# FFN1 of two token groups in one pass over the weights, FFN2 one pass later, output gates before decay gates

## The reference, cut to what matters

```python
def reference(x, ...):                       # x: 16 x 2048 x 1024, float32
    # macaron half-step FFN before mixing (FFN1, hidden width 2816)
    h = rms_norm(x, ffn1_norm[l])
    x = x + 0.5 * swiglu(h, ffn1_w_gate[l], ffn1_w_up[l], ffn1_w_down[l])
    # two head groups from one projection
    h = rms_norm(x, mix_norm[l])
    proj = h @ w_in[l]
    fq, fk, fv, ff, gq, gk, gv, g_low, g_out = jnp.split(proj, split_idx, axis=-1)
    log_f = jax.nn.log_sigmoid(ff + fox_forget_bias[l])
    fox = fox_attention(fq, fk, fv, log_f)                 # 8 heads, causal, over all earlier frames
    log_a = jax.nn.log_sigmoid(g_low @ gla_w_gate_up[l] + gla_gate_bias[l]) / 16
    gla = gla_chunk_causal(gq, gk, gv, log_a)              # 4 heads, chunks of 64, a running state
    gla = rms_norm(gla, gla_out_norm[l]) * jax.nn.silu(g_out)
    x = x + jnp.concatenate([fox, gla], axis=-1) @ w_out[l]
    # macaron half-step FFN after mixing (FFN2)
    h = rms_norm(x, ffn2_norm[l])
    x = x + 0.5 * swiglu(h, ffn2_w_gate[l], ffn2_w_up[l], ffn2_w_down[l])
    return rms_norm(x, final_norm)
```

## Time and profile before

| | |
|---|---|
| median of 6 runs | 2874.18 us (2869.43 to 3200.55) |
| profiled execution | 2870.64 us |
| its span on the slowest core | 2869.1 us (cores 2850.7 to 2869.1 us) |
| TensorE busy | 2678.3 us, 93% of the span, 13328 matmuls |
| VectorE, ScalarE, GpSimd busy | 1468.1, 1103.9, 250.8 us |
| mean granted TensorE clock, cores 0 to 7 | 0.981 to 0.985 |
| moved by DMA | 423.20 MB; read from HBM 451.09 MB, written 59.77 MB |

### The profile page before, as it was taken

The page is one execution under the profiler, slowest core; times in us unless marked ns, Lnnn a source line. Parts: engine busy times, 40 slices in busy tenths (PEclk is TensorE's granted clock), DMA queues, the critical chain, the costliest instruction groups (busy, mean ns, idle before and its releaser), DMA issues.

```text
span 2869.1 us, 40029 instructions; the slowest of 8 cores (2850.7 to 2869.1 us)
## 1 busy us (share of the span) xinstructions
PE 2678.3 (93%) x13328; PEld 1262.1 (44%) x13328; DVE 1468.1 (51%) x2186; ACT 1103.9 (38%) x2189; POOL 250.8 (9%) x518
## 2 busy tenths in 40 slices
PE   5989888898899999999999999999999999999998
PEld 2435434443345444544445444454444544544443
DVE  3353772582445554456444863547444566455443
ACT  1231431461224732267322531326323375277211
POOL 1111211120000100001000100001000010001000
PEclk9999999999999999999999999999999999999999
DMA  8888769869777454433444354442644423433453
GB/s 182 137 162 157 159 136 184 175 169 222 181 181 191 123 187 145 140 107 121 157 138 141 121 156 167 129 139 89 199 144 136 129 93 125 143 93 126 136 170 115
DMA packets 128166, 423.20 MB, mean 148 GB/s; under 512 B 14799, under 2 KB 14944, under 8 KB 127072
## 3 DMA queue, kind: packets, MB, share of 16 engines
q1 hardware_dynamic: 95920, 308.34, 32.9%
q0 software_dynamic: 31760, 111.26, 22.0%
q10 hardware_dynamic: 288, 1.05, 0.1%
HBM read 451.09 MB, written 59.77 MB: 178 GB/s over the span
## 4 chain that ended last, share of the span: by engine, by line
PE 76%; DMA 10%; DVE 8%; issue 4%; ACT 2%; POOL 0%; DVEq 0%; SPq 0%; ACTq 0%; POOLq 0%
PE bank L303 76%; DMA mixw_t<-mixw 4%; DMA wgu<-wgu 2%; DVE hF L343 2%; DVE hM L740 2%; DVE x_sb L343 1%; DMA wgu<-wgus 1%; DVE Sst L343 1%; DMA wd<-wd 1%; DVE hM L343 1%; DVE Sbf L340 1%; ACT L328 1%; DVE thF L343 1%; DMA wgus<-wgu 1%; DMA mixws<-mixw_t 1%
## 5 line engine op out<-in xcount | busy, mean ns | idle before, releaser
L303 PE MATMUL bank<-hF,wgu 128*128 128x512 bf16 x5632 | 1297.3, 384 | 73.7 <-DMA wgu<-wgu 27.6
L303 PEld LDWEIGHTS bank<-hF,wgu 128*128 128x128 bf16 x5632 | 548.4, 99 | 743.0 <-issue 128.2
L303 PE MATMUL bank<-act,wd 128*128 128x512 bf16 x2816 | 648.8, 381 | 29.5 <-DVE x_sb L343 22.7
L328 ACT ACTIVATE thF<-bank 128x512 f32<-128x512 f32 x352 | 209.7, 598 | 847.0 <-PE bank L303 846.0
L343 DVE SCALAR_TENSOR_TENSOR thF<-thF,bank 128x512 f32<-128x512 f32 x352 | 240.9, 686 | 509.1 <-ACT thF L328 506.8
L328 ACT ACTIVATE hM<-bank,biasT 128x256 bf16<-128x256 f32 (+1 forms) x1152 | 437.8, 472 | 126.6 <-PE bank L303 126.1
L303 PEld LDWEIGHTS bank<-act,wd 128*128 128x128 bf16 x2816 | 272.3, 98 | 362.8 <-issue 52.2
L340 DVE TENSOR_TENSOR act<-bank,thF 128x512 bf16<-128x512 f32 x352 | 242.6, 689 | 188.3 <-PE bank L303 182.6
L343 DVE SCALAR_TENSOR_TENSOR x_sb<-bank,x_sb 128x512 f32<-128x512 f32 x256 | 173.7, 689 | 319.2 <-PE bank L303 318.0
L740 DVE RECIPROCAL hM<-bank 64x128 f32<-64x128 f32 x256 | 244.4, 955 | 52.0 <-PE bank L303 35.1
L340 POOL TENSOR_TENSOR hM<-hM,mask 128x128 bf16<-128x128 bf16 x256 | 118.4, 475 | 1514.9 <-ACT hM L328 1514.5
(11 more groups left out here) (92 smaller groups left out, 1260.3 us busy)
## 6 DMA issues: line engine op xcount, KB each, us to landing
wgu<-wgus SPq DMA_DIRECT2D x264, 512.0 KB, 3.5
wd<-wds SPq DMA_DIRECT2D x192, 352.0 KB, 3.1
wgu<-wgu POOLq DMA_DIRECT2D x88, 512.0 KB, 7.4
mixw_t<-mixws SPq DMA_DIRECT2D x88, 512.0 KB, 3.4
wd<-wd POOLq DMA_DIRECT2D x64, 352.0 KB, 6.7
wgus<-wgu SPq DMA_DIRECT2D x44, 512.0 KB, 5.4
mixw_t<-mixw POOLq DMA_DIRECT2D x40, 512.0 KB, 7.7
wds<-wd SPq DMA_DIRECT2D x32, 352.0 KB, 5.6
```

The costliest lines, as they stand in the source:

```text
L303: ins = e.matmul(out, lhsT=l, rhs=r, start=s0, stop=s1)
L328: ins = e.activation(out=out, in_=in_, func=func, **kw)
```

## The change

FFN1 of groups 0 and 1 becomes one pass (`ffn1_pair`). `ffn` takes a list of lanes (input, activation buffers, group); each weight tile is loaded once and used for every lane. The pair's second lane keeps its input `hF2` and activations `act2` in the tensor `V` (the attention's values, not used before mixer 0), so the fill of V's constant columns moves behind the pair. In the pair's first half the first three tiles are done for lane 0, then for lane 1, and from there on by turns. `x` of group 1 is loaded behind group 0's, and its sums of squares are taken ahead of the pair. Both mixers 0 and 1 then stand behind the pair, and the passes go f1(2), f2(0), f2(1), f1(3), f2(2), ... as before from there on.

`LOADW` now stores every FFN1 tile and every mixer chunk at its first use; FFN2 is as before. Only the first down tile of a half is cut into 10 and 1, and its parts are no longer woven with the second tile's. In the mixer, the four projections of the output gate (chunks 0 and 1) stand ahead of the decay gates.

```diff
@@ build_nc
+        flat = V[:].rearrange("p a b c -> p (a b c)")
+        hF2 = flat[:, 0:8 * T].rearrange("p (k t) -> p k t", k=8)
+        act2 = flat[:, 8 * T:(8 + NC2) * T].rearrange("p (k t) -> p k t", k=NC2)
...
-        MSET(V[:, :, :, 64:128], 1.0, [("V", p, g) for p in range(4) for g in range(4)], eng="dve")
@@ LOADW
-        def LOADW(tag, wb, tile, src, keep, i, first, reads=()):
+        def LOADW(tag, wb, tile, src, keep, i, spread, reads=()):
...
-            kept_at = first + i % 2
+            kept_at = i % 2 if spread else 0
@@ ffn
+        def ffn(f, lanes, middle):
+            pair = len(lanes) == 2
             for half in range(2):
+                todo = [(c, L) for c in range(NC2) for L in lanes]
+                if pair and half == 0:
+                    todo = [(c, L) for L in lanes for c in range(3)] + todo[6:]
+                where = {}
+                for cl, L in todo:
+                    if cl not in where:
+                        where[cl] = wb = nxt("wgu", 3)
+                        LOADW("wgu", wb, wgu[:, wb, :], wgu_d[f], wgu_s[f], half * NC2 + cl, f,
+                              [("x", 0, 5)] if cnt["wgu"] <= 3 else ())
+                    wb = where[cl]
...
-                load(0)
-                load(1)
-                part(0, 0, NC2 - 1)
-                part(1, 0, NC2 - 1)
-                part(0, NC2 - 1, NC2)
-                evac(0)
-                part(1, NC2 - 1, NC2)
-                evac(1)
...
+                for d in range(8):
+                    wb = nxt("wd", 4)
+                    LOADW("wd", wb, wd[:, wb, :], wd_d[f], wd_s[f], half * 8 + d, f, [("act", 5)] if cnt["wd"] <= 4 else ())
+                    for L in lanes:
+                        b = ring[n % 2]
+                        n += 1
+                        for c0, c1 in ([(0, NC2 - 1), (NC2 - 1, NC2)] if d == 0 else [(0, NC2)]):
+                            MM(banks[b][:], [(wd[:, wb, c * 128:(c + 1) * 128], L.act[:, c, :]) for c in range(c0, c1)],
...
+                        STT(x_sb[:, L.xb, d, :], banks[b][:], 0.25, x_sb[:, L.xb, d, :], ALU.mult, ALU.add, [],
+                            [PS(b), ("x", L.xb, d)], level=0)
@@ ffn1_pair
+            norm_h(0, 0, rstdF[:], "rstdF", hF, "hF", 0.5)
+            norm_h(1, 0, rstdM[:], "rstdM", hF2, "hF2", 0.5)
+            ffn(0, [Lane(0, hF, "hF", act, "act", sums(0, sqF, "sqF"), 6),
+                    Lane(1, hF2, "hF2", act2, "act2", sums(1, sqM, "sqM"), 7)], middle)
+            norm_rstd(rstdM[:], "rstdM", 6, 0)
+            norm_h(0, 1, rstdM[:], "rstdM", hM, "hM", 0.5)
+            norm_rstd(rstdF2[:, 1], ("rstdF2", 1), 7, 0.5)
+            MSET(V[:, :, :, 64:128], 1.0, [("V", p, g) for p in range(4) for g in range(4)]
+                 + [("hF2", k) for k in range(8)] + [("act2", c) for c in range(NC2)], eng="dve", level=0.7)
@@ mixer: the loop over chunks 0 and 1 (output gates) moves from behind biasT to ahead of zb
-                LOADW("mixw", wb, mixw[:, wb, :], mixw_d, mixw_s, i, 1, [("act", 10)] if cnt["mix"] <= 2 else ())
+                LOADW("mixw", wb, mixw[:, wb, :], mixw_d, mixw_s, i, 0, [("act", 10)] if cnt["mix"] <= 2 else ())
@@ the order of the passes
-        order = [("f1", 0), ("f1", 1)]
-        for g in range(NTG - 3):
+        P.level = 2
+        ffn1_pre(0, 2, sqF, "sqF", rstdF[:], "rstdF")
+        load_x(1, [("x", 0, 7)])
+        ffn1_pre(1, 3, sqM, "sqM", rstdM[:], "rstdM")
+        load_x(2, [("act", 8)])
+        ffn1_pair(pre(2))
+        P.level = 1
+        mixer(0)
+        norm_h(1, 1, rstdF2[:, 1], ("rstdF2", 1), hM, "hM", 0.5)
+        mixer(1)
+        order = [("f1", 2), ("f2", 0)]
+        for g in range(1, NTG - 3):
             order += [("f2", g), ("f1", g + 2)]
...
-            m = g if kind == "f1" and g < NTG - 1 else NTG - 1 if (kind, g) == ("f2", NTG - 3) else None
+            m = {("f2", 0): 2, ("f2", NTG - 3): NTG - 1}.get((kind, g), g if kind == "f1" and 2 < g < NTG - 1 else None)
```

More of the change, by code:

```diff
@@ L456, in ffn @@
                     STT(thF[:, r, :], thF[:, r, :], 1.0, banks[bg][:], ALU.add, ALU.mult, [], [PS(bg), ("th", r)], level=0)
-                    TT(act[:, cl, :], banks[bu][:], thF[:, r, :], ALU.mult, [("th", r)], [PS(bu), ("act", cl)], level=0)
+                    TT(L.act[:, cl, :], banks[bu][:], thF[:, r, :], ALU.mult, [("th", r)], [PS(bu), (L.atag, cl)], level=0)
                 ring = [(bu + 1) % 3, (bu + 2) % 3]
                 cnt["fb"] = bu + 1
[L460 to L478, removed]
@@ L480, in ffn @@
-                load(0)
-                load(1)
-                part(0, 0, NC2 - 1)
-                part(1, 0, NC2 - 1)
-                part(0, NC2 - 1, NC2)
-                evac(0)
-                part(1, NC2 - 1, NC2)
-                evac(1)
[L488 to L493, removed]
-            return bu
+                n = 0
@@ new lines, in ffn @@
+                for d in range(8):
[6 more added lines that the diff above has]
+                            MM(banks[b][:], [(wd[:, wb, c * 128:(c + 1) * 128], L.act[:, c, :]) for c in range(c0, c1)],
+                               [("wd", wb)] + [(L.atag, c) for c in range(c0, c1)], [PS(b)], start=(c0 == 0),
+                               stop=(c1 == NC2))
+                        STT(x_sb[:, L.xb, d, :], banks[b][:], 0.25, x_sb[:, L.xb, d, :], ALU.mult, ALU.add, [],
+                            [PS(b), ("x", L.xb, d)], level=0)
+                        if half == 1:
+                            L.after(d, bu if L.bank is None else L.bank)
+                    if d == 1 and half == 0 and middle is not None:
+                        middle(bu)
@@ L496, in ffn1, with sums @@
+            return bu
+        def sums(xb, sq, tag):
+            return lambda d, b: norm_sq(xb, d, sq, tag, b, d == 7, 0)
         def ffn1(tg, middle):
@@ L498, in ffn1, with ffn1_pair, load_x, ffn1_pre @@
             norm_h(xb, 0, rstdF[:], "rstdF", hF, "hF", 0.5)
-            b = ffn(0, xb, lambda d, b: norm_sq(xb, d, sqF, "sqF", b, d == 7, 0), middle)
+            b = ffn(0, [Lane(xb, hF, "hF", act, "act", sums(xb, sqF, "sqF"))], middle)
             norm_rstd(rstdM[:], "rstdM", b, 0)
             norm_h(xb, 1, rstdM[:], "rstdM", hM, "hM", 0.5)
-        def load_x(tg):
-            xb = tg % 3
[L505 to L512, removed]
+        def ffn1_pair(middle):
+            norm_h(0, 0, rstdF[:], "rstdF", hF, "hF", 0.5)
[7 more added lines that the diff above has]
+                 + [("hF2", k) for k in range(8)] + [("act2", c) for c in range(NC2)], eng="dve", level=0.7)
+        def load_x(tg, reads=()):
+            xb = tg % 3
+            DMA("sp" if tg < 3 else "pool", ("x", xb, tg < 3), x_sb[:, xb, :, :].rearrange("p k t -> p (k t)"), x_d[tg],
+                1 << 21, reads=reads, writes=[("x", xb, k) for k in range(8)], slack=8000.0)
+        def ffn1_pre(tg, b, sq, tag, rstd, rtag):
             for k in range(8):
-                norm_sq(xb, k, sqF, "sqF", b, k == 7, None)
-            norm_rstd(rstdF[:], "rstdF", b, None)
+                norm_sq(tg % 3, k, sq, tag, b, k == 7, None)
+            norm_rstd(rstd, rtag, b, None)
         def ffn2(tg, middle):
@@ L563, in mixer, with ev @@
             ACTV([(fa, fa, AF.Exp, None, -1.0)], [], ["fa"])
+            for i in range(2):
+                w3, wk = chunk(i)
+                for hh in range(2):
+                    h = 2 * i + hh
+                    def ev(b, h=h):
+                        ACTV([(t1f, banks[b][:], AF.Tanh, None, 0.5)], [], [PS(b), ("sqM", 0), ("sqM", 1)])
+                        STT(cc[:, 4 + h, :], t1f, 1.0, banks[b][:], ALU.add, ALU.mult, [("sqM", 0), ("sqM", 1)],
+                            [PS(b), ("cc", 4 + h)])
+                    proj_T(w3, wk, hh * 128, ev)
             zb = []
@@ L611, in mixer @@
                    ALU.subtract, ["fref"] + [("nFs", g) for g in range(tg + 1)], [("biasT", t)])
[L612 to L619, removed]
-                            [PS(b), ("cc", 4 + h)])
-                    proj_T(w3, wk, hh * 128, ev)
             w3, wk = chunk(2)
```

24 lines of the change are left out of this document (11 added, 13 removed).

## The result

The changed kernel takes 2782.04 us (median of 10 runs, 2776.89 to 3228.09) against 2874.92 (median of 20) of the kernel before on the same chip: ratio 0.9671, 95% interval 0.9644 to 0.9698. The forecast was 2788. Executions in which a die ran at a lower clock are in the medians and ranges but not in the ratios; one experiment (the rewoven down tiles) had too few others for a ratio, so two single times stand for it. The profiled execution took 2784.26 us, its span 2782.3 on core 1.

What follows compares the result with a forecast made beforehand. TensorE was taken as the bound. Loss up to f1(3)'s end falls from 169 to 91.5 us; that 77.5 and 8 behind it take 2870.6 to 2785, median 3.5 above: 2788 us, range 2745 to 2845.

Steps and rivals of the forecast that it cites:

- Start of the pair: Up to the end of lane 1's first three tiles at 56.6 us: loss 35 us, bounds 27 and 54.
- with all eight behind it I add 4: Pair's start: all eight squares of group 1 follow x's landing, adding an estimated 4 us to the 4.7 before the norm.
- Rest of the pair: Pair behind its start: loss 5 us for the turns between halves, bounds 0 and 20.
- rival 3: Pair bound by DMA: at 9 us per tile it costs 40 us, giving 2828 us; chance 0.04.
- Mixer 0: Mixer 0 under f1(2): loss 25 us, from V's fill 3, the chunk ring 12 and latencies 10.
- Mixer 1: Mixer 1 under f2(0), with chunks in bfloat16: loss 14 us over 230 us, against 42 before.
- mixer 2, f2(1), f1(3): Stage with no float32 chunk left: loss 12.5 us; bounds together with mixer 1, 20 and 40.
- Down tiles: Unwoven down tiles behind f1(3): 8 us gained of 14.4 us of eviction waits; bounds 14 gained, 10 lost.
- Output gates: Output gates first in mixers 1 to 7: costed at nothing, or a microsecond per mixer if evictions hold up banks.
- Rival 1: Only the 66.7 us of weight waits go, other loss stays, new waits add 28: 2835 us; chance 0.10.
- Rival 2: Chunk ring decides, 14 us per further microsecond per chunk: 2843 at mixer 1's rates; chance 0.10 with gain, 0.06 without.
- Rival 4: Change doesn't spread: fixed order holds work behind late weights, mixers 1 and 2 lose as before: 2826 us; chance 0.04.

Runs made afterwards that it cites:

- Experiments 7: Changed kernel with group 1's x sent first, group 2's in the pair's middle, first four down tiles one per hidden tile: 2778.25 us, ratio 0.9641 to the kernel before.
- 10: On top of experiment 7's edits, group 1's squares and sums at the highest level and its load's slack 0: 2775.86 us, ratio 0.9614 to the kernel before.
- the second set: Changed kernel and kernel before, both unaltered, measured again on another chip: 2784.25 against 2881.45 us, ratio 0.9668.
- experiment 6: Changed kernel with the mixer's chunks stored at their second or third use again, FFN1's tiles as changed: 2813.32 us, ratio 0.9767 to the kernel before.
- experiment 4: Changed kernel with the output gates projected behind the decay gates again: ratio 0.9726 to the kernel before, 16 us slower than the changed kernel.
- experiment 5: Changed kernel with single-lane down tiles woven again and output gates back behind the decay gates: 2830.12 us, ratio 0.9825 to the kernel before.
- Experiment 9: Kernel before with one edit, the output gates projected ahead of the decay gates: ratio 0.9991 to the kernel before.
- (1): Changed kernel with the pair taken apart, lane 1 a second pass that loads the stored tiles again: 2824.11 us, ratio 0.979 to the kernel before.

## Why the prediction came out, step by step

The total is right, and the loss goes where it was said to go, but the terms are not right: one large term was too big and two small ones too small. That they met within 6 us is luck.

*Start of the pair* (loss 35, measured 37.9). Of its steps, the third tile was to land near 35 and did at 34.7. But the first tile was the one waited for, and it landed at 27.2: I had priced the last of three loads that share the bandwidth. x landed at 28.3, earlier than my 31. The step that failed is the one behind it, "with all eight behind it I add 4": the squares didn't follow the landing, they stand among lane 0's tiles. Hence 51.5 instead of 46 (the steps as written add up to 45). Experiments 7 and 10 show this: an earlier x alone leaves the 8.8 us wait, an earlier place in the order halves it.

*Rest of the pair* (5, bounds 0 and 20; measured 9). A burst came back, without x in it: four down tiles sent at 82.6 to 84.1, and the `wgu` load behind them landed after 18.8 us. Everything else in the pair ran without a loss, at a DMA share of 0.67 to 0.9, so rival 3 is out.

*Mixer 0* (25, measured 21.1; 31.2 for pair and order alone). The chunk loads took a median of 7.2 us, as taken, and TensorE waited 8.5 us for them (11.5 in the second set) where 12 were forecast; experiment 6 prices the stores at 8. By the Trainium skill, "DMA: Bandwidth & Descriptors", section "Anatomy of one DMA", the estimate was 4.4 us for a load and no wait at all; no load came under 5.0, and the measurement decides. That section is on DMAs issued from GpSimd; the 3.2 us for a store by SyncE's queue went beyond it, and the 14 stores took 2.6 to 8.1 us, 5.3 in the median. The latencies, put at 10, were larger without the output gates' move, which shortened them: the wait on `cc` in mixer 0 is 2.8 us here and 10.0 in experiment 4.

*Mixer 1* (14, measured 10.4; alone 15.1) and *mixer 2, f2(1), f1(3)* (12.5, measured 15.5; alone 28.4). The second is the mis-sized term: I took the late rate and the rate of 778 to 1135 us and then went below both. Nor were the chunks from the scratch free: 7.0 of these 15.5 us are waits on them. Alone the two lose 43.5, more than the upper bound of 40 that I gave them. f1(3) ends at 1064 us instead of 1134 (1057 forecast), but 1091 in experiment 5: pair, storing and order move that end by 43 us, not 77.5, and the rest comes from the next two parts.

*Down tiles* (8, measured 28 and, alone, 25). Step "of 14.4 us I take 8": all of it went, since an eviction behind three norms is in time for the bank, and none of the feared cost came (`thF` waits 16.7 and 18.8). And it holds ahead of f1(3) as well: over the whole run `x_sb` waits went from 22.7 to 0.7 us, which I had counted only behind f1(3). The rest of the 28 is not one wait; other small waits shrank with it, and I have no row that says why.

*Output gates* ("I cost it at nothing", measured 16). I asked whether the projections were hidden and not what they could hide: they are work that is ready where the next mixer's decay gates are not, and from the second place they put attention off. Experiment 9 shows that this needs the new order.

So 77.5 + 8 + 0 was forecast, and 50 + 28 + 16 came. How the 50 divide is open: taken out of the whole, sharing is worth 35 (1) and the chunks' early stores 29 (6), which is more than 50 already, so these parts lean on each other; and no run takes out the order of passes, or the early stores of FFN1's tiles in the pair, alone. Of the marks given ahead: the pair's end came at 285, not 275; waits on float32 `wgu` and chunks are 26.9 us (25 forecast), but two thirds are in the pair, not in mixer 0, and the 10.3 for chunks from the scratch stand beside them; PEclk behind 300 us is 0.98 to 1.00. Rival 1 (2835) is out, since 45 of the 75 us gained up to f1(3) are losses beside the waits on weights. Rival 2's mechanism exists at 8 us. Rival 4 was half right: without the two small edits the order spreads less than it says.

## What to carry to other kernels

When engines run a fixed order, price a moved operation by what it lets others fill as well as by what covers it, and by what it stands in front of; the same move was worth 16 us here in the new order and nothing in the old. Of several loads that go out together, price the first one needed, since it pays for all of them; and ask of a late input whether its consumers stand at the landing or behind other work in the order. A total that comes out is no proof of its terms: take the parts apart, each alone and all but each.

## What the hardware showed that was not expected

Of three float32 `wgu` tiles that went out beside two loads of x (2 MB each), none landed in less than 14.8 us, against 9.2 before with the same tiles and one load of x; behind four down tiles one took 18.8, though x was not in flight. And a gap costs more than its length: the 5.7 us wait at 104 us was followed by matmuls of 0.44 us, and the window from 95 to 110 us had 0.78 of the clock.
